# First modulation made by column quarters, with the first four projection tiles summed k-outer behind it

## What is computed

```
c_act = jax.nn.silu(c)
mod = (c_act @ w_ada[l] + b_ada[l])[:, None, :]
sh1, sc1, gt1, sh2, sc2, gt2 = jnp.split(mod, 6, axis=-1)
h = rmsnorm(x, g_norm1[l]) * (1 + sc1) + sh1
(a_q, a_kv, i_q, i_k, i_w, b_q, ...) = split_cols(h @ w_in[l], IN_SPLITS)
```

## Time and profile before

| | |
|---|---|
| median of 3 runs | 1064.98 us (1062.2 to 1067.61) |
| profiled execution | 1068.17 us, its span 1066.2 us |
| mean granted TensorE clock of the profiled execution | 0.977 |
| busy share of the span | PE 94%, DVE 45%, ACT 39%, POOL 11% |

### The profile page before, as it was taken

How to read it: one execution, slowest core, us unless ns; L and a number is a source line. 1 busy time by engine, 2 the same in 40 slices (tenths; PEclk the granted TensorE clock), 3 DMA queues, 4 the chain that set the end, 5 groups by cost and what they waited for, 6 DMA issues and landing times.

```text
span 1066.2 us, 12661 instructions
## 1 busy us (share of the span) xinstructions
PE 997.5 (94%) x4831; PEld 808.3 (76%) x4831; DVE 484.5 (45%) x803; ACT 412.5 (39%) x676; POOL 115.5 (11%) x136
## 2 busy tenths in 40 slices
PE   2469999999999999999999999799999999999997
PEld 0457888877877676777888888678888888788886
DVE  4363577863335335546546368543323323322331
ACT  4143533235555555642222222253434443312231
POOL 3000000000025431200000007300000000001111
PEclk9679999999999999999999999799999999999999
DMA  8933232521122101043565692123232233223312
GB/s 313 369 96 96 65 104 92 148 89 60 40 92 87 61 22 40 30 142 117 181 203 186 207 335 80 40 79 111 85 118 79 82 115 100 87 79 109 104 35 79
DMA packets 93262, 121.49 MB, mean 114 GB/s; under 512 B 4680, under 2 KB 83109, under 8 KB 93090
## 3 DMA queue, kind: packets, MB, share of 16 engines
q1 hardware_dynamic: 92690, 114.67, 32.5%
q0 software_dynamic: 528, 6.22, 1.9%
HBM read 118.20 MB, written 8.45 MB: 119 GB/s over the span
## 4 chain that ended last, share of the span: by engine, by line
PE 88%; DMA 3%; DVE 2%; ACT 2%; SPq 2%; issue 1%; POOL 0%; POOLq 0%; DVEq 0%; ACTq 0%
PE tile_ps L761 25%; PE tile_ps L763 24%; PE tile_ps L762 24%; DMA w_raw<-in_w_in_dram 3%; PE s_ps L901 2%; PE o_ps L948 2%; PE t_ps L919 2%; SPq L517 1%; PE s_ps L904 1%; PE tile_ps L962 1%; PE tile_ps L1007 1%; PE tile_ps L968 1%; PE tile_ps L1008 1%; PE tile_ps L1009 1%; DVE w_lo L1437 1%
## 5 line engine op out<-in xcount | busy, mean ns | idle before, releaser
L761 PE MATMUL tile_ps<-h_hi,w_hi 128*128 128x512 f32 x816 | 326.1, 400 | 29.2 <-DVE h_lo L1477 21.4
L763 PE MATMUL tile_ps<-h_hi,w_lo 128*128 128x512 f32 x816 | 319.5, 392 | 0.0
L762 PE MATMUL tile_ps<-h_lo,w_hi 128*128 128x512 f32 x816 | 319.3, 391 | 0.0
L1437 DVE TENSOR_TENSOR w_lo<-w_raw,w_hi 128x2048 fp32r<-128x2048 f32 (+2 forms) x78 | 172.3, 2209 | 257.5 <-ACT w_hi L1142 257.5
L761 PEld LDWEIGHTS tile_ps<-h_hi,w_hi 128*128 128x128 f32 x816 | 153.6, 188 | 73.8 <-issue 34.0
L1142 ACT ACTIVATE w_hi<-w_raw 128x2048 fp32r<-128x2048 f32 (+2 forms) x78 | 143.9, 1844 | 98.3 <-PE tile_ps L763 67.1
L763 PEld LDWEIGHTS tile_ps<-h_hi,w_lo 128*128 128x128 f32 x816 | 153.6, 188 | 33.3
L762 PEld LDWEIGHTS tile_ps<-h_lo,w_hi 128*128 128x128 f32 x816 | 153.8, 189 | 29.9
L761 PE MATMUL tile_ps<-f_hi,w_hi 128*128 128x512 f32 x176 | 68.6, 390 | 2.5 <-DVE f_lo L1861 2.5
L763 PE MATMUL tile_ps<-f_hi,w_lo 128*128 128x512 f32 x176 | 68.5, 389 | 0.0
L762 PE MATMUL tile_ps<-f_lo,w_hi 128*128 128x512 f32 x176 | 68.5, 389 | 0.0
(11 more groups left out here) (272 smaller groups left out, 1356.2 us busy)
## 6 DMA issues: line engine op xcount, KB each, us to landing
w_raw<-in_w_in_dram SPq DMA_DIRECT2D x31, 1024.0 KB, 5.3
...
row_copies<-row_flat POOLq DMA_DIRECT2D x1, 5632.0 KB, 22.8
...
```

The lines of the kernel that those rows point to most:

```text
L761: pe.matmul(tile_ps[b][0:mw, :], wh, x_hi[:, kx, :], start=start, stop=False)
L762: pe.matmul(tile_ps[b][0:mw, :], wh, x_lo[:, kx, :], start=False, stop=False)
L763: mm = pe.matmul(tile_ps[b][0:mw, :], wl, x_hi[:, kx, :], start=False, stop=stop)
L1437: dve.tensor_tensor(w_lo[s][:, 0:kt, :], w_raw[s][:, 0:kt, :], w_hi[s][:, 0:kt, :].bitcast(F32), ALU.subtract) \
```

## The change

- The two 1024-wide groups of `w_ada` become four quarters q of 256 columns, each with shift and scale columns (`ada1`, `ada1_sc`): 4 transfers a quarter of 4 k-tiles by 256 columns. SP's order becomes quarter 0, weight chunk 0, quarter 1, chunk 1, quarters 2 and 3, chunk 2.
- DVE sums only 7 of the 8 k-tiles (`add_quarter`); the last goes straight to PE as a second matmul per column (`mod_quarter`). After each quarter DVE makes two columns of `amp1` (`amplitude`) and two k-tiles of `h_lo` (`hidden_lo`).
- `h` is not written over `x_T` any more: ACT makes `h_hi` from `x_T` with scale and bias (`hidden_hi`), POOL makes the full `h` in two buffers `h_full`, DVE subtracts.
- PE runs tiles 0 to 3 in four banks (`query_ps`), k-outer, between the quarters (`query_part`). The splits of tiles 0 to 3 read those banks.
- The scaling of `x_nat` is shared: blocks 0 and 1 on ACT, 2 and 3 on DVE; ACT's copies of the bias rows stand before it.
- POOL issues `row_copies` after `h_ready` has reached 8.
- The counts of `mod_made` for the later groups fall by two.

```diff
-            for g in range(2):
-                for k in range(KT):
-                    sp.dma_start(ada1[g][k][:], a["w_ada"][0][k * P:(k + 1) * P, g * D:(g + 1) * D]) \
-                        .then_inc(ada1_in[g][k], 16)
-            load(0, [(KT, 0, cols(COL_IQ, CW))])
-            load(1, [(KT, 0, cols(COL_IQ + CW, CW))])
+            for q in range(4):
+                for j in range(2):
+                    for g, dst in enumerate((ada1, ada1_sc)):
+                        c0 = g * D + q * CW
+                        sp.dma_start(dst[q][j][:], a["w_ada"][0][4 * j * P:4 * (j + 1) * P, c0:c0 + CW]
+                                     .rearrange("(k p) n -> p k n", p=P)).then_inc(ada1_in[q][j], 16)
+                if q < 2:
+                    load(q, [(KT, 0, cols(COL_IQ + q * CW, CW))])
...
+            for kt in range(KT):
+                pool.wait_ge(amp_ready, kt // 2 + 1)
+                pool.wait_ge(xt_read, kt + 1)
+                if kt >= 2:
+                    pool.wait_ge(h_ready, kt - 1)
+                pool.tensor_scalar(h_full[kt % 2][:], x_T[:, kt, :], amp1[:, kt:kt + 1], shift1[:, kt:kt + 1],
+                                   ALU.mult, ALU.add).then_inc(h_full_made, 1)
             pool.wait_ge(rows_stored, 16 * 4)
+            pool.wait_ge(h_ready, KT)
             pool.dma_start(rep_dram, row_dram.to_broadcast([P, FL_W])).then_inc(rows_copied, 16)
...
-            for g in range(2):
-                pe.wait_ge(ada1_added, KT * (g + 1))
-                mod_columns(ada1_sum[g], 8, 8 * g)
-
-            project_two(0, 0, ready=h_ready)
-            project_two(1, 2)
+            def mod_quarter(q):
+
+                pe.wait_ge(ada1_added, (KT - 1) * (q + 1))
+                pe.wait_ge(ada1_in[q][1], 32)
+                for g, last in enumerate((ada1, ada1_sc)):
+                    for m in range(2):
+                        o = mod_ps[:, 8 * g + 2 * q + m:8 * g + 2 * q + m + 1]
+                        pe.matmul(o, ada1_sum[q][:, g, m * P:(m + 1) * P], ones[:, 0:1], start=True, stop=False)
+                        mm = pe.matmul(o, last[q][1][:, 3, m * P:(m + 1) * P], c_act[:, KT - 1:KT], start=False,
+                                       stop=True)
+                mm.then_inc(mod1_made, 1)
...
+            for kt in range(4):
+                turn_x(kt)
+            mod_quarter(0)
+            for kt in range(4, KT):
+                turn_x(kt)
+            chunk_ready(0)
+            for t in range(2):
+                query_part(t, range(0, 2))
+            mod_quarter(1)
+            for t in range(2):
+                query_part(t, range(2, 4))
+            mod_quarter(2)
+            chunk_ready(1)
+            pe.wait_ge(xt_read, 6)
+            for t in range(2, 4):
+                query_part(t, range(0, 4))
+            for t in range(4):
+                query_part(t, range(4, 6))
+            mod_quarter(3)
+            for t in range(4):
+                query_part(t, range(6, 8))
...
+            for q in range(4):
+                add_quarter(q)
+                amplitude(q)
+                if q == 0:
+                    make_lo(0)
+                hidden_lo(q)
+                if q == 1:
+                    make_lo(1)
```

More of the change, by code:

```diff
@@ L590, in load_ada2 @@
                 if j < 2:
-                    sp.wait_ge(mod_made, n + 2)
+                    if n:
+                        sp.wait_ge(mod_made, n)
                 else:
@@ L794, in _, with turn_x @@
             pe.wait_ge(brow_out, 3)
-            for kt in range(KT):
+            def turn_x(kt):
                 if kt >= 4:
@@ L800, in _, with query_part @@
                 mm.then_inc(xt_made, 1)
-            for g in range(2):
-                pe.wait_ge(ada1_added, KT * (g + 1))
-                mod_columns(ada1_sum[g], 8, 8 * g)
-            project_two(0, 0, ready=h_ready)
-            project_two(1, 2)
+            def mod_quarter(q):
[8 more added lines that the diff above has]
+                mm.then_inc(mod1_made, 1)
+            def query_part(t, kts):
+                s, m0 = t // 2, t % 2 * P
+                for kt in kts:
+                    pe.wait_ge(h_ready, kt + 1)
+                    wh, wl = w_hi[s][:, kt, m0:m0 + P], w_lo[s][:, kt, m0:m0 + P]
+                    pe.matmul(query_ps[t][:], wh, h_hi[:, kt, :], start=kt == 0, stop=False)
+                    pe.matmul(query_ps[t][:], wh, h_lo[:, kt, :], start=False, stop=False)
+                    mm = pe.matmul(query_ps[t][:], wl, h_hi[:, kt, :], start=False, stop=kt == KT - 1)
+                if KT - 1 in kts:
+                    mm.then_inc(tile_made[t % 2], 1)
+            for kt in range(4):
[19 more added lines that the diff above has]
+                query_part(t, range(6, 8))
             project_two(2, 4, mw=(P, 72))
@@ L1448, in _ @@
             link(dve.tensor_tensor(c_act, c_exp, c_col, ALU.mult))
[L1450 to L1453 removed]
+            dve.wait_ge(x_sq, NBLK)
+            dve.tensor_scalar(ms_x, ms_x, EPS, None, ALU.add).then_inc(pow_in, 1)
+            dve.wait_ge(pow_out, 1)
+            for b in range(2, NBLK):
+                dve.tensor_scalar(x_nat[:, b, :], x_nat[:, b, :], rs_x[:, b:b + 1], None, ALU.mult) \
+                    .then_inc(x_scaled, 1)
@@ L1461, in _ @@
-                    if n == 1:
-                        dve.wait_ge(x_sq, NBLK)
-                        dve.tensor_scalar(ms_x, ms_x, EPS, None, ALU.add).then_inc(pow_in, 1)
-            make_lo(0)
-            dve.wait_ge(mod_made, 2)
-            link(dve.tensor_tensor(mod[:, 0:16], mod_ps[:, 0:16], b_ada[:, 0:16], ALU.add))
-            link(dve.scalar_tensor_tensor(out=amp1, in0=scale1, scalar=1.0, in1=g_n1, op0=ALU.add, op1=ALU.mult))
-            dve.wait_ge(xt_read, KT)
-            for kt in range(KT + 1):
-                if kt < KT:
-                    dve.tensor_scalar(x_T[:, kt, :], x_T[:, kt, :], amp1[:, kt:kt + 1], shift1[:, kt:kt + 1],
-                                      ALU.mult, ALU.add).then_inc(h_full_made, 1)
-                if kt:
-                    k = kt - 1
-                    dve.wait_ge(h_hi_made, k + 1)
-                    dve.tensor_tensor(h_lo[:, k, :], x_T[:, k, :], h_hi[:, k, :].bitcast(F32), ALU.subtract) \
-                        .then_inc(h_ready, 1)
@@ L1479, in _, with amplitude @@
-            make_lo(1)
+                    for g, (total, w) in enumerate(for_both):
+                        if k:
+                            ins = dve.scalar_tensor_tensor(out=total, in0=w, scalar=c_act[:, k:k + 1], in1=total,
+                                                           op0=ALU.mult, op1=ALU.add)
+                        else:
+                            ins = dve.tensor_scalar(total, w, c_act[:, 0:1], None, ALU.mult)
+                    ins.then_inc(ada1_added, 1)
+            def amplitude(q):
+                dve.wait_ge(mod1_made, q + 1)
+                for g in range(2):
+                    c0 = 8 * g + 2 * q
+                    ins = dve.tensor_tensor(mod[:, c0:c0 + 2], mod_ps[:, c0:c0 + 2], b_ada[:, c0:c0 + 2], ALU.add)
+                link(ins)
+                dve.scalar_tensor_tensor(out=amp1[:, 2 * q:2 * q + 2], in0=scale1[:, 2 * q:2 * q + 2], scalar=1.0,
+                                         in1=g_n1[:, 2 * q:2 * q + 2], op0=ALU.add, op1=ALU.mult).then_inc(amp_ready, 1)
@@ new lines, in hidden_lo @@
+            def hidden_lo(q):
+                for kt in (2 * q, 2 * q + 1):
+                    dve.wait_ge(h_hi_made, kt + 1)
+                    dve.wait_ge(h_full_made, kt + 1)
+                    dve.tensor_tensor(h_lo[:, kt, :], h_full[kt % 2][:], h_hi[:, kt, :].bitcast(F32), ALU.subtract) \
+                        .then_inc(h_ready, 1)
+            for q in range(4):
[6 more added lines that the diff above has]
+                    make_lo(1)
```

66 lines of the change are left out of this document (40 added, 26 removed).

## The result

| | before | changed |
|---|---|---|
| median, us | 1064.98 | 1074.29 (1071.71 to 1076.12) |
| ratio to before | | 1.0083, 95% interval 1.0059 to 1.0106 |
| profiled execution / its span | 1068.17 / 1066.2 | 1076.12 / 1073.1 |
| mean granted clock | 0.977 | 0.973 |
| tile 4 begins | 86.27 | 89.83 |

The changed kernel is slower by 0.8%, 6 to 11 us. In the profiled executions tile 5 begins 6.55 us later, and the whole span is 6.9 longer. Behind tile 5 the difference hardly changes: PE's granted clock was low for a shorter time near 680 and once more near 940 (0.83 in the window 936 to 946), which gave back 1.2 us and cost 1.6. The medians are 9.3 apart. The profiled execution of before was 3.2 above its median, that of the changed kernel 1.8 above; what makes the rest of the difference between 6.9 and 9.3 no trace shows.

The account below looks back on a forecast made before the run. PE carries 88% of the chain, but the first 90 us wait for weight chunk 0's transfer. The chain's terms put tile 4 at 87.4 against 86.27, 1.1 us later: 1064.98 + 1.1 = 1066, range 1059 to 1072.

Parts of the forecast that it names:

- The transfer wait: Before the first tile: some 18 us of waiting for weight chunk 0 under the bias-row copy would go away.
- The power: Start of the chain, POOL after DVE adds eps: power out at 17.7, DVE free from scaling at 19.1.
- One quarter's sums: DVE's sums over a quarter of the modulation weights: 6.2 us each, 25 us for four.
- the far bound: Upper bound on DVE's sums for a quarter: 6.5 us, with 0.10 between dependent sums.
- cheaper sums: Rival: DVE's sums take 4.6 us a quarter by the skill's formula; tile 4 4.8 us earlier, 1061; chance 0.07.
- Columns: PE's eight matmuls per quarter: 3.6 us for quarters 0 and 2, 2.7 for quarter 1, 1.85 for quarter 3.
- h: After a quarter's amp1, ACT, POOL and DVE make two k-tiles: 2.6 us; quarter 0 adds 0.5 for POOL beside DVE.
- The 48 matmuls: PE's work on tiles 0 to 3 ahead of the last columns: 12.7 us, nine matmuls at half clock.
- The stall ahead of tile 4: PE waits for the splits of chunk 2 and tile 2: from tile 3's end, DVE is done at 4.35 us.
- The clock: PE's gaps before k-tiles 6 and 7 and before tile 4: one fall charged, nine matmuls 0.2 slower, 1.8 us.
- the mark: The start of tile 4, 86.27 before, where the sum stopped; behind it the program is the same.
- the clock low and POOL blocked: Rival: clock low throughout and POOL blocks DVE; 6.4 us more, tile 4 at 93.8, 1072.5; chance 0.15.

Follow-up runs that it names:

- b1: The kernel before with one edit: the copy of the bias rows waits until h is complete; 1051.89 us, ratio 0.9869.
- b4: The changed kernel with matmuls whose results nobody reads placed in PE's waits; 1067.98 us, ratio 1.0021 to before.
- d1: The changed kernel with DVE adding the next quarter before it waits for a quarter's columns, and PE's last columns right behind quarter 2's; 1068.36 us.
- d2: d1 with PE's order following: last columns after tiles 2 and 3 for k-tiles 0 to 3, then tiles 0 and 1 ended first; 1057.96 us.
- e1: d2 with matmuls of no use in PE's two waits left ahead of the last columns; 1054.73 us, ratio 0.9892 to before.

## Why the prediction was wrong

The places of the loss were right, its size was wrong. 1066.0 was said, 1074.29 came, above the range's 1072. Point by point:

- **The transfer wait.** Right: 18 us, and it goes; b1 shows 17.5. The loads moved at about 350 GB/s (351 from 20 to 30, 345 from 30 to 44), not 387; nothing waited for them.
- **The power.** Right: DVE scales at 17.75 and is free at 19.08 (17.7 and 19.1 said).
- **One quarter's sums.** 6.5, the far bound, not 6.2: the dependent start is 0.10 behind the end, as in the seven 1024-wide sums of the earlier trace rows, and not the 0.04 of two others in that group. 0.9 over quarters 0 to 2. The estimate of 4.6 took a formula of which the same section of the Trainium skill (VectorE: DVE Perf Modes) says that it under-predicts. Its rival, cheaper sums, did not come.
- **Columns.** 2.0, 3.6, 3.6 and 1.85 against 3.6, 2.7, 3.6 and 1.85. The errors partly cancel: up to quarter 2 the columns took 0.7 less in sum, the sums 0.9 more and the rest 0.3 more, so the columns of quarter 2 end at 59.2 (58.7 said).
- **h.** 2.7 behind the last amp1, 2.6 said. In quarter 0 POOL and DVE collide by more than the 0.5 taken. Timeline of POOL in the changed kernel, quarters 0 and 1:

```profile
28.17 4.00 POOL L691 TENSOR_SCALAR h_full<-x_T,cst 128x512 f32<-128x512 f32 x2 [7.88 <-DVE cst L1554]
43.61 1.52 POOL L691 TENSOR_SCALAR h_full<-x_T,cst 128x512 f32<-128x512 f32 x2 [11.43 <-DVE cst L1554]
```

  The pair takes 4.00 (2.73 beside DVE's split of chunk 0, 1.28 beside the first h_lo) and 1.52 in quarter 1, where DVE stood still for most of it; DVE's split kept its 2.28, and DVE then waited 0.74 and 0.58 for POOL. The Trainium skill (SBUF — State Buffer, "Who interferes with whom") names this pair of instructions as one that contends; the trace agrees. Which side pays differs: in quarter 0 POOL, 2.5 us; in quarters 2 and 3 DVE, whose two h_lo take 1.78 beside POOL, where quarter 1 has 1.36.
- **The 48 matmuls.** 13.9, not 12.7: the low clock lasted over 14 of them, not nine. The last columns began at 73.04 (71.4 said), 1.6 late.
- **The stall ahead of tile 4.** 4.31 measured, 4.35 said.
- **The clock. This is the step that failed**: "PE's gap before k-tiles 6 and 7 and this one are each near 4 us of little work; I charge one fall of the clock, nine matmuls 0.2 slower, 1.8". There were two, of 2.4 and 3.0, together 5.4, and the second lies in tile 4 itself, behind the mark at which the sum stopped. The two waits had been found and sized; only one fall was charged, at nine matmuls, where 11 and 14 ran slow.

Late at tile 5 are 6.55 us, where 1.1 were said. The missing 5.4 are 0.5 from DVE's chain up to the columns of quarter 2, 1.1 from the 48 matmuls, 3.0 from the fall in tile 4, and 0.8 from the fall ahead of it. b4 shows the kind: with PE kept busy tile 5 begins 8.7 earlier and the same kernel takes 6.3 us less. This accounts for the traces. The median of before and 6.55 make 1071.5, still inside the range; the last 2.8 up to 1074.29 lie between medians and profiled executions, and their cause stays open. The rival that came nearest had the clock low and POOL blocked, 1072.5 with 0.15.

What the sum did not do at all was to price the parts of the change apart. It took the wait of 18 us as gone and spent it at once on the quarters. Had it asked what the late copy gives by itself, the 18 us of wait stood in its own rows; b1 measured 17.4 at tile 4 and 13.5 in the median. d1 and d2 show what most of the 22.4 us of the quarters are: PE and DVE waiting for one another. The two orders take back 16.3, and the clock in PE's first waits 1.6 to 3.2. The remaining 2.8 between e1 and b1 are within what the intervals leave open, though tile 4 is 4.0 later in e1's profiled execution.
